# A decoder trunk in float32: the first layer's memory keys and values by seven quarter-block products each

## What is computed

```python
def memory_cross_attention(h, mem_n, wq, wkv, wo):
    B, S, D = h.shape
    q = (h @ wq).reshape(B, S, X_HEADS, X_DH)
    k, v = jnp.split(mem_n @ wkv, 2, axis=-1)
    ...
    p = jax.nn.softmax(s, axis=-1)
    o = jnp.einsum('bhsm,bmhd->bshd', p, v.astype(F32)).reshape(B, S, D)
    return o.astype(h.dtype) @ wo

for l in range(DEPTH):
    h = rms_norm(x, norm_mix[l])
    ...
    x = x + memory_cross_attention(rms_norm(x, norm_cross[l]), rms_norm(mem, norm_mem[l]),
                                   wq_x[l], wkv_x[l], wo_x[l])
    x = x + hierarchical_moe(...)
```

## Time and profile before

| | us |
|---|---|
| median of three runs | 1037.96 |
| the profiled execution, its own time | 1038.54 |
| its span in the trace | 1036.4 |
| PE busy | 1005.5 (97% of the span) |
| DVE busy | 474.2 (46%) |
| ACT busy | 135.7 (13%) |
| POOL busy | 98.6 (10%) |
| DMA, mean over the span | 283 GB/s |

### The profile page before, as it was taken

The page is one execution under the profiler, slowest core; times in us unless marked ns, Lnnn a source line. Parts: engine busy times, 40 slices in busy tenths (PEclk is TensorE's granted clock), DMA queues, the critical chain, the costliest instruction groups (busy, mean ns, idle before and its releaser), DMA issues.

```text
span 1036.4 us, 11068 instructions
## 1 busy us (share of the span) xinstructions
PE 1005.5 (97%) x4500; PEld 549.7 (53%) x4500; DVE 474.2 (46%) x782; ACT 135.7 (13%) x307; POOL 98.6 (10%) x123
## 2 busy tenths in 40 slices
PE   8999999999999999999999999999999999998896
PEld 7657556669574453343334855565964433342332
DVE  2533375766443224332444626485654444443343
ACT  2211001412010011100111000041111011100111
POOL 3051032000010000000000602210000100000000
PEclk9999999999999999999999999999999999999999
DMA  9954001844469999999999320084385799999995
GB/s 359 424 203 154 9 1 43 367 163 159 166 256 372 417 423 419 421 422 421 421 421 420 118 81 1 1 332 182 135 350 226 309 422 419 421 422 419 422 415 196
DMA packets 44825, 293.57 MB, mean 283 GB/s; under 512 B 5472, under 2 KB 5728, under 8 KB 13024
## 3 DMA queue, kind: packets, MB, share of 16 engines
q1 hardware_dynamic: 38000, 266.36, 63.1%
q10 hardware_dynamic: 5616, 22.24, 5.6%
q0 software_dynamic: 1152, 4.19, 1.0%
HBM read 283.33 MB, written 9.44 MB: 282 GB/s over the span
## 4 chain that ended last, share of the span: by engine, by line
PE 88%; DMA 4%; SPq 3%; DVE 2%; issue 1%; ACT 1%; POOL 0%; DVEq 0%; POOLq 0%; ACTq 0%
PE bank L975 17%; PE bank L1040 9%; PE bank L573 8%; PE bank L603 5%; PE bank L769 5%; PE bank L605 5%; PE bank L583 5%; PE bank L1010 5%; PE bank L826 5%; PE bank L890 5%; PE bank L676 5%; PE bank L698 3%; DMA ring<-in_w_experts 3%; PE bank L563 2%; DMA late<-in_w_experts 2%; SPq L536 2%
## 5 line engine op out<-in xcount | busy, mean ns | idle before, releaser
L975 PE MATMUL bank<-ring,hT 128*64 128x512 f32 x688 | 197.1, 594 | 5.2 <-DMA ring<-in_w_experts 5.2
L975 PEld LDWEIGHTS bank<-ring,hT 128*64 128x64 f32 x688 | 61.8, 137 | 106.4 <-issue 94.8
L573 PE MATMUL bank<-ring,hT 128*128 128x512 f32 x192 | 84.4, 592 | 0.0
L1010 PE MATMUL bank<-PT 128*128 128x512 f32 x128 | 59.2, 605 | 0.0
L1898 DVE TENSOR_TENSOR x<-bank,x 128x512 f32<-128x512 f32 x64 | 44.2, 691 | 29.0 <-PE bank L1010 29.0
L573 PEld LDWEIGHTS bank<-ring,hT 128*128 128x128 f32 x192 | 35.6, 190 | 40.2 <-issue 40.2
L1040 PE MATMUL bank<-ring,xs 128*64 128x512 f32 x224 | 56.7, 595 | 0.0
L1908 DVE TENSOR_SCALAR PT<-columns,wsm 128x128 f32<-128x128 bf16 x32 | 11.0, 343 | 99.6 <-PE bank L1040 91.2
L583 PE MATMUL bank<-hT,ring 128*128 128x256 f32 x256 | 55.7, 379 | 0.8 <-DVE hT L1538 0.8
L769 PE MATMUL bank<-ring,hT 128*128 128x512 f32 x128 | 56.3, 595 | 0.0
L583 PEld LDWEIGHTS bank<-hT,ring 128*128 128x128 f32 x256 | 48.6, 190 | 8.0 <-issue 1.4
(11 more groups left out here) (294 smaller groups left out, 1546.0 us busy)
## 6 DMA issues: line engine op xcount, KB each, us to landing
ring<-in_w_experts SPq DMA_DIRECT2D x140, 1024.0 KB, 15.3
ring<-in_w_mix SPq DMA_DIRECT2D x60, 1024.0 KB, 16.4
work<-in_w_experts SPq DMA_DIRECT2D x24, 1024.0 KB, 16.0
late<-in_w_experts SPq DMA_DIRECT2D x10, 1024.0 KB, 24.1
keys<-in_w_experts SPq DMA_DIRECT2D x10, 1024.0 KB, 26.1
late<-in_w_mix ACTq DMA_DIRECT2D x4, 2048.0 KB, 10.0
rot<-by_slot ACTq DMA_DIRECT2D x14, 512.0 KB, 7.9
ring<-in_w_experts SPq DMA_DIRECT2D x12, 512.0 KB, 15.9
```

What stands on the lines that cost most here:

```text
L573: last = nc.tensor.matmul(b[:, :], lhs[:, c, m * P:(m + 1) * P], w[:, c, :], start=(c == 0), stop=(c == C - 1))
L975: last = nc.tensor.matmul(banks[2 + g][b2 * CAP:(b2 + 1) * CAP, :], rows_T_of(p)[:, c, b2 * CAP:(b2 + 1) * CAP], w, start=(c == 0), stop=( ...
L1010: routed_job(nc.tensor.matmul(banks[OUT_BANK[n][m]][:, :], gatedT[:, m, :], yrows[:, n * W:(n + 1) * W], start=True, stop=True))
```

## The change

It makes the first layer's keys and values by seven quarter products each. The 2x2 blocks are halves of the memory tokens by halves of the weights' rows and columns. A key job is now 16 products of 128 columns, a value job 4 products of 512 columns; there are 14 jobs (`MEM_JOBS`) in place of eight, and several add onto a bank that an earlier one has left (`MEM_ONTO`). The four sums of memory blocks and eight sums of weight blocks (128x2048 each) are made on DVE, as are six additions of a bank to what ACT or DVE stored (`add_mem`). `ksums` and `vsums` get a slot of the ring each, so `hf` now waits for slot 0. On ACT the bounds' exponential and the rotary sines stand behind the copies of keys, and on POOL the multiplication of the kept memory stands behind the norm of x and waits for all weight sums. The ten identity products take the place of fourteen.

```diff
-SUMS, Q_SUMS, P_SUMS = "sums", "qsums", "psums"
-SUMS_AFTER = {"av": SUMS, "q1": Q_SUMS, "p1": P_SUMS}
+SUMS, Q_SUMS, P_SUMS, K_SUMS, V_SUMS = "sums", "qsums", "psums", "ksums", "vsums"
+SUMS_AFTER = {"av": SUMS, "q1": Q_SUMS, "p1": P_SUMS, "k1": K_SUMS, "v1": V_SUMS}
+MEM_JOBS = [f"k_{i}" for i in (1, 2, 6, 5, 7, 3, 4)] + [f"v_{i}" for i in (1, 5, 6, 3, 7, 2, 4)]
+MEM_BANK = {"k": {1: 0, 6: 0, 7: 0, 4: 0, 5: 1, 3: 1, 2: 2}, "v": {1: 7, 6: 7, 7: 7, 4: 7, 5: 3, 3: 3, 2: 6}}
+MEM_ONTO = {6: 1, 7: 6, 4: 7, 3: 5}
+MEM_BY = {1: "A", 6: "A", 5: "A", 4: "A", 2: "D", 7: "D", 3: "D"}
...
-            for _ in range(14):
+            for _ in range(10):
...
-            pe.wait_ge(mem_gained, 3)
+            def mem_seventh(name):
...
+                if i in (1, 2):
+                    wait_loaded(pe, 0, f"{u}0", i - 1)
+                if i == 3:
+                    wait_loaded(pe, 0, f"{u}1", 1)
+                if name in ("k_1", "k_2"):
+                    pe.wait_ge(mem_gained, i)
+                if sums_at:
+                    pe.wait_ge(mem_token_sum, sums_at)
+                if weights_at:
+                    pe.wait_ge(mem_weight_sum, 4 * "kv".index(u) + weights_at)
+                if i in MEM_ONTO:
+                    wait_mem_emptied(pe, f"{u}_{MEM_ONTO[i]}")
...
                 if L == 0:
-                    for j in range(8):
-                        if j == 4:
+                    for name in MEM_JOBS:
+                        if name == "v_1":
                             pe.wait_ge(mem_kept, 4)
-                        kv_job(j, banks[j], unit(UNITS[j // 2]), hT, parts=lambda half: wait_loaded(pe, L, UNITS[j // 2], half))
+                        mem_seventh(name)
...
                 if L == 0:
+                    keep_mem("k_1", 0, 0)
+                    keep_mem("k_6", 0, 1)
+                    keep_mem("k_5", 1, 1)
                     act.wait_ge(x_loaded, 16)
                     squares(6 * L)
-                    for j in range(8):
-                        empty_kv(L, j, banks[j])
+                    keep_mem("k_4", 1, 0)
+                    act.wait_ge(lb_max, 1)
+                    nc.scalar.activation(gains[:, :, 36:40], gains[:, :, 36:40], ACT.Exp).then_inc(lb_exp, 1)
+                    act.wait_ge(trig_arg, 1)
+                    nc.scalar.activation(cosT[:, :, :], cosT[:, :, :], ACT.Sin)
+                    nc.scalar.activation(sinT[:, :, :], sinT[:, :, :], ACT.Sin).then_inc(tables_done, 1)
+                    keep_mem("v_1", 0, 0)
+                    keep_mem("v_5", 1, 1)
+                    keep_mem("v_6", 0, 1)
+                    keep_mem("v_4", 1, 0)
...
                 norm(0)
+                if L == 0:
+                    pool.wait_ge(gains_loaded, 16)
+                    pool.wait_ge(mem_kept, 4)
+                    pool.wait_ge(mem_weight_sum, 8)
...
+            dve.wait_ge(mem_gained, 4)
+            mem_tokens(1, rows_block(1, 0), rows_block(1, 1), ALU.add)
+            mem_tokens(2, token_sums(0), rows_block(0, 0), ALU.subtract)
+            mem_loads("k", 0)
+            mem_weights("k", 1, kt1, k12, k11)
+            mem_loads("k", 1)
+            mem_weights("k", 2, kt2, k22, kt1)
+            mem_tokens(3, rows_block(0, 0), rows_block(1, 0), ALU.subtract)
+            mem_tokens(4, rows_block(0, 1), token_sums(1), ALU.subtract)
+            add_mem("k_2", 0, 0, "k_1")
+            mem_weights("k", 3, k12, k22, k12)
+            dve.wait_ge(mem_jobs, MEM_NTH["k_1"])
+            mem_weights("k", 4, k11, k21, kt2)
+            for half in range(2):
+                mem_loads("v", half)
+            mem_weights("v", 1, vt1, v12, v11)
+            add_mem("k_7", 1, 1, "k_5")
+            add_mem("k_3", 0, 1, "k_6")
+            mem_weights("v", 2, vt2, v22, vt1)
+            mem_weights("v", 3, v12, v22, v12)
...
             last.then_inc(gains_done, 1)
+            dve.wait_ge(mem_jobs, MEM_NTH["v_1"])
+            mem_weights("v", 4, v11, v21, vt2)
+            add_mem("v_3", 0, 1, "v_6")
+            add_mem("v_7", 1, 1, "v_5")
...
                 for m in range(M):
                     scale_tile(L, 0, m)
+                if L == 0:
+                    add_mem("v_2", 0, 0, "v_1")
```

More of the change, by code:

```diff
@@ L112, in bank_plan @@
     return bank_of, before
+MEM_JOBS = [f"k_{i}" for i in (1, 2, 6, 5, 7, 3, 4)] + [f"v_{i}" for i in (1, 5, 6, 3, 7, 2, 4)]
+MEM_NTH = {name: i + 1 for i, name in enumerate(MEM_JOBS)}
+MEM_BANK = {"k": {1: 0, 6: 0, 7: 0, 4: 0, 5: 1, 3: 1, 2: 2}, "v": {1: 7, 6: 7, 7: 7, 4: 7, 5: 3, 3: 3, 2: 6}}
+MEM_ONTO = {6: 1, 7: 6, 4: 7, 3: 5}
+MEM_BY = {1: "A", 6: "A", 5: "A", 4: "A", 2: "D", 7: "D", 3: "D"}
+MEM_EMPTIED = {name: sum(MEM_BY[int(n[2])] == MEM_BY[int(name[2])] for n in MEM_JOBS[:i + 1]) for i, name in enumerate(MEM_JOBS)}
+MEM_LAST = {"k0": "k_4", "k1": "k_3", K_SUMS: "k_4", "v0": "v_4", "v1": "v_7", V_SUMS: "v_4"}
+BANK_LAST = {0: "k_4", 1: "k_3", 2: "k_2", 3: "v_3", 4: "v_3", 5: "v_3", 6: "v_2", 7: "v_4"}
 BANK, BANK_BEFORE = bank_plan(["router_kv0", "router_kv1"])
@@ L624, in _ @@
                     last.then_inc(mem_tr, 1)
-            pe.wait_ge(mem_gained, 3)
+            def mem_seventh(name):
+                u, i = name[0], int(name[2])
+                sums = {"k": K_SUMS, "v": V_SUMS}[u]
+                rows_at, sums_at, weights, weights_at = {
+                    1: (rows_block(0, 0), 0, weight_block(0, f"{u}0", 0), 0), 2: (rows_block(0, 1), 0, weight_block(0, f"{u}0", 1), 0),
+                    5: (token_sums(0), 1, weight_block(0, sums, 0), 1), 6: (token_sums(1), 2, weight_block(0, sums, 1), 2),
+                    7: (token_sums(2), 3, weight_block(0, f"{u}1", 0), 3), 3: (token_sums(3), 4, weight_block(0, f"{u}1", 1), 0),
+                    4: (rows_block(1, 1), 0, weight_block(0, f"{u}0", 0), 4)}[i]
+                if i in (1, 2):
[10 more added lines that the diff above has]
+                    wait_mem_emptied(pe, f"{u}_{MEM_ONTO[i]}")
+                b, fresh = mem_bank(name), i not in MEM_ONTO
+                if u == "k":
+                    for n in range(4):
+                        for c in range(4):
+                            last = nc.tensor.matmul(b[:, n * P:(n + 1) * P], weights[:, c, n * P:(n + 1) * P], rows_at[:, c, :],
+                                                    start=(fresh and n == 0 and c == 0), stop=(n == 3 and c == 3), skip_group_check=not fresh)
+                else:
+                    for c in range(4):
+                        last = nc.tensor.matmul(b[:, :], rows_at[:, c, :], weights[:, c, :], start=(fresh and c == 0), stop=(c == 3),
+                                                skip_group_check=not fresh)
+                last.then_inc(mem_jobs, 1)
@@ L1000, in rows_transposes @@
                         if L + 1 < DEPTH:
[L1001 removed]
+                            pe.wait_ge(kv_emptied, min(p - 2 + ROUTER_KV, LOOP_KV - 1) + 1 if p > 1 else ROUTER_KV)
                     for k in range(4):
```

74 lines of the change are left out of this document (48 added, 26 removed).

## The result

The changed kernel takes **1040.93 us** (median of 8 runs, 1040.4 to 1042.22) against 1037.97 (8 runs) for the kernel before: 2.96 us more, ratio 1.0028 with an interval of 1.0019 to 1.0037. The interval leaves out 1, so the change is slower, by 0.19 to 0.37%. The profiled execution took 1040.86.

A forecast was written before the change was run, and what follows sets the result against it. The prediction took PE, busy 1005.5 of 1036.4 us, as the bound. +0.4 us at v_4 and +0.45 at the scaling put `hf` +0.9 us later: median 1037.96 + 0.9 = 1038.9 us, range 1036.8 to 1041.2.

The forecast's parts named there:

- (b): PE's stall ahead of k_4: clock falls to half, costing 3.2 us, giving 1039.6 us; chance 0.12 for over 2.1 us.
- (c): Load of `v1`: it lands after 34.58 us, delaying all behind it one for one; at 2 us, 1040.9; chance 0.10.
- DVE's queue: Last value job v_4 waits for DVE's fourth value sum and addition of v_7; ends at 67.3, 0.4 us later.
- GpSimd's hold: DVE's scaling of x is held until POOL's memory multiplication ends at 66.1; scaling ends at 67.5, costing 0.45 us.
- The start: Fewer identity products: a gain of 0.4 us that does not last, as k_6 starts about 18.8 to 19.5.
- The landing and the stall: `v1` lands at 34.58, DVE lets k_4 go at 37.7, PE stands 4.6 us; most of its 6.3 us saving goes.
- k_4's length: Key job k_4, behind PE's stall: taken at 3.57 us, full clock.
- ACT's wait: v_6 waits for ACT's copy of v_1 behind the sines, ending at 49.1, where PE is ready at 48.2: 0.9 us.
- Later work: POOL's sums run about 75 to 89, holding DVE's work on `hf` back some 4 us, covered by 10.65 us idle.
- The shift passes undiminished: From the start of `hf` to the end: a shift there, forecast +0.9 us, should reach the end undiminished.
- Rival (a): Keys and values: DVE keeps pace, so PE's 6.30 us and 0.4 at the start show, 1031.3 us; chance 0.08.

The follow-up runs named there:

- e10_restored: The changed kernel with 227 small DVE copies in layer 0's arm that is not executed, moving its layer 1 code to a whole 256-instruction shift; median 1039.70 us.

## Why the prediction was right, and where not

The time, 1040.93, lies in the range (1036.8 to 1041.2), but 2.0 us over the forecast, and by a little in the outcome held at 0.22, that of rivals (b) and (c). The profiled execution took 2.32 us more than the one before (1040.86 - 1038.54), where 0.9 was forecast. That the range held is in part luck: the two terms that made the 0.9, DVE's queue at v_4 and GpSimd's hold, set nothing in this execution, and two that the sum lacked, the clock and the branch, happened to be small. Step by step:

- **The start** held (the prediction reads half clock for the identity products from their pace of 0.226 us; the profile's granted clock there is 1.00, so that reading is open): no gain by fewer identity products, and k_6 at 19.16 (18.8 to 19.5 forecast), after a wait for DVE's second key sum.
- **The landing and the stall** held: `v1` at 34.65 (34.58), k_4 at 37.93 (37.7). Most of PE's 6.3 us went here, as told.
- **k_4's length** failed. The sum had 3.57 us at full clock; it took 6.49. This is rival (b), held at 0.12 on the evidence of the earlier trace rows, which were misread. They are a gap of the chain, from 290.5 to 294.29, and not of PE, which worked through most of it. PE's timeline of the kernel before:

```profile
290.33 1.04 PE L563 MATMUL bank<-ident,xs 128*128 128x128 f32 x8
291.97 1.91 PE L910 MATMUL bank<-hT,og 128*20 128x128 f32 x16 [0.60 <-DVE hT L1538]
294.29 1.09 PE L563 MATMUL bank<-ident,xs 128*128 128x128 f32 x8 [0.42 <-DVE xs L1528]
```

Its longest wait there was 0.60 us, and behind its first products its longest in the whole trace was 1.3, so the trace of the kernel before had nothing to say on a wait of 4 us. The wait here was 4.2 us, v_6's in the kernel with k_7 first 5.5, and k_4's in the padded one (`e10_restored`) 5.3; all three lowered the clock. The rule on HAM oscillation in the Trainium skill, "TensorE: Matmul & The Clock Gate", was the better guide, though the clock also fell behind waits of 2.10 and 2.49 us, shorter than the gaps that it names. The loss, 2.9 us, was near the 3.2 that I priced; PE alone then ended the values at 68.46 (68.5 by the rival).
- **ACT's wait** at v_6 was hidden: the copy of v_1 started at 48.02 (48.5 forecast), and PE came later.
- **DVE's queue** was sized right (additions done at 63.59; 63.85 forecast), and hidden by the late PE: no value job waited here, though the prediction's sign was PE idle for about 1 us ahead of v_4. Where the clock held behind the stall, it did set the end: v_4 at 64.2 to 64.9 in three kernels, with `v1` landing at 35.1 to 35.8.
- **GpSimd's hold** was as forecast (scalings done at 67.26; 67.5) and hidden too. Its 0.45 us appeared in no run.
- So **`hf`** came at 70.97, by the clock, where I had 70.3 by DVE and POOL: 0.67 us more.
- **Later work** was covered: POOL's three sums began at 77.58, and DVE still stood idle for 9.86 us ahead of the addition that answers to the one at 104.27.
- **The shift passes undiminished** failed by 0.72 us in this execution, by up to 1.65 in others. I had looked for work that could absorb a shift, and not for anything that a longer program could add. `hf`'s 1.57 and this 0.72 make 2.29 of the 2.32 us. The medians differ by 2.96; the other 0.6 lies between executions, and no trace shows it.
- **Rival (c)** was partly real: `v1` landed between 34.65 and 36.14 us in the profiles of the kernels that kept the change's order, and DVE followed it one for one. Whether the small load's early issue is to blame was not tried.
- **Rival (a)** did not come in this order, for the reason given; in another order it did, with `hf` 5.72 us sooner.

## What to carry over

When arithmetic is traded for additions on another engine, list what each engine's queue holds behind its first wait for a late load: here bounds, angles and masks, which nothing kept from running sooner, decided between 3 us lost and 2 to 3 us won (4.5 with the code's place restored as well). Price a stall of about 4 us of an otherwise busy TensorE at the stall plus some 3 us lost to the lower clock, and allow for 1.6 us lost behind one of 2 us or a little more. Before a gap in the chain is taken for a gap of an engine, look at that engine's timeline. And where a program branches at run time just ahead of a stretch bound by DMA, measure a change also with the code padded back to its old place, since the place alone moved this kernel by 1 to 1.6 us.

## What the runs showed of the hardware that I had not expected

- Copies that are never executed made a kernel slower (1.6 us in the median), by DVE's idle time at a branch: 3.85 to 4.59 us or 5.03 to 5.83, by where the branch lies, with one or two transfers of code in it. A shift by 256 instructions in all brought the shorter time back.
- TensorE's granted clock was 0.57 in the 6.5 us behind a wait of 4.2 us. It also fell behind waits of 2.10 and 2.49 us (0.87 on average from 20 to 33 us), and stayed at 1.00 behind others of 1.45 to 1.95 and one of 2.17.
- The issue of one load of 256 KB occupied ACT's queue for 4.5 to 6.1 us (line 1215, at 13 to 14 us) while 4 MB of zeros and the weights were under way; the kernel before issued it at 28.05 in 0.33 us. ACT copied nothing meanwhile.
- The landing of the second half of `v1` moved by 1.5 us (34.65 to 36.14) between kernels that issue it alike, at 6.3 to 7.0 us.
